# Block 1's back projection as seven half-size products, weight sums made in block 0's heads, and gamma and beta applied in the first state-space tiles

## The reference, cut to what matters

```python
def reference(x, ...):                    # x is 1 x 512 x 2048, fp32
    x = first_block(x, ...)
    return second_block(x, ...)

def first_block(x, w_in, ..., w_out, ln_g, ln_b):
    ...                                    # attention (8 heads), short convolution, pooling
    y = einsum('bse,ed->bsd', y, w_out)    # back projection, 512 x 2048 times 2048 x 2048
    return layer_norm(ALPHA * x + y, ln_g, ln_b)

def second_block(x, w_in, w_out, ..., ln_g, ln_b):
    ...                                    # sparse attention (8 heads), state-space mixer (4 groups)
    sub = einsum('bse,ed->bsd', mixed, w_out)
    return layer_norm(ALPHA_2 * h + sub, ln_g, ln_b)
```

## Time and profile before

| | us |
|---|---|
| median of 3 runs (1691.88 to 1692.17) | 1692.14 |
| the profiled execution's own time | 1692.62 |
| its span, first to last instruction | 1690.9 |
| PE busy in the span | 1677.5 (99%) |
| DVE, ACT, POOL busy | 914.2, 665.4, 716.4 |
| PE's granted clock, mean over the span | 0.998 |

### The profile page before, as it was taken

One profiled execution on the slowest core, in us unless ns is written; L12 is line 12 of the kernel. 1 busy time (PEld: TensorE's weight loads), 2 busy tenths in 40 slices (PEclk: granted clock), 3 DMA queues, 4 the chain that ended last, 5 costly groups with the idle time before them and its releaser, 6 DMA issues.

```text
span 1690.9 us, 21775 instructions
## 1 busy us (share of the span) xinstructions
PE 1677.5 (99%) x7902; PEld 1376.8 (81%) x7902; DVE 914.2 (54%) x1373; ACT 665.4 (39%) x917; POOL 716.4 (42%) x304
## 2 busy tenths in 40 slices
PE   9999999999999999999999999999999999999997
PEld 6888888888888888888888888887668888888886
DVE  6323312332455654988642754748789745556326
ACT  6434434443222225446642333424453545462220
POOL 4433343433444443446554434334235333326551
PEclk9999999999999999999999999999999999999999
DMA  6333233332577844765554342433123222217422
GB/s 238 114 93 92 89 93 94 93 94 82 202 289 292 296 150 139 244 229 185 172 172 156 92 134 87 137 105 119 61 77 100 75 87 75 87 50 275 135 89 100
DMA packets 67360, 232.31 MB, mean 137 GB/s; under 512 B 7336, under 2 KB 7592, under 8 KB 66000
## 3 DMA queue, kind: packets, MB, share of 16 engines
q1 hardware_dynamic: 59184, 206.33, 37.5%
q10 hardware_dynamic: 8096, 24.88, 4.1%
HBM read 205.93 MB, written 25.25 MB: 137 GB/s over the span
## 4 chain that ended last, share of the span: by engine, by line
PE 99%; DVE 1%; DMA 0%; issue 0%; SPq 0%; ACT 0%; DVEq 0%; ACTq 0%
PE bank L575 96%; PE bank L579 2%; DVE feats L1568 0%; DMA feats<-in_x_t 0%; DVE bank L1948 0%; DVE stats L1906 0%; DVE planes_lo L1579 0%; DVE planes_lo L1955 0%; ACT planes_hi L1105 0%; SPq L399 0%; SPq L401 0%; DVE mv L1935 0%; DVE rstd L1924 0%; DVEq L1933 0%; DVEq L1945 0%
## 5 line engine op out<-in xcount | busy, mean ns | idle before, releaser
L525 POOL TENSOR_TENSOR w_lo<-raw,w_hi 128x1024 fp32r<-128x1024 f32 x280 | 693.0, 2480 | 934.8 <-ACT w_hi L1060 934.8
L575 PE MATMUL bank<-planes_hi,w_hi 128*128 128x512 f32 (+1 forms) x1776 | 694.7, 391 | 1.1 <-ACT planes_hi L1105 0.7
L575 PE MATMUL bank<-planes_hi,w_lo 128*128 128x512 f32 (+1 forms) x1776 | 685.3, 386 | 0.0
L575 PE MATMUL bank<-planes_lo,w_hi 128*128 128x512 f32 (+1 forms) x1776 | 684.7, 386 | 0.1
L1060 ACT ACTIVATE w_hi<-raw 128x1024 fp32r<-128x1024 f32 x302 | 320.5, 1061 | 866.4 <-PE bank L575 813.0
L575 PEld LDWEIGHTS bank<-planes_hi,w_hi 128*128 128x128 f32 x1776 | 333.7, 188 | 84.2 <-issue 17.2
L575 PEld LDWEIGHTS bank<-planes_hi,w_lo 128*128 128x128 f32 x1776 | 333.6, 188 | 67.9
L575 PEld LDWEIGHTS bank<-planes_lo,w_hi 128*128 128x128 f32 x1776 | 333.9, 188 | 66.9 <-DVE planes_lo L1579 1.3
L575 PE MATMUL bank<-w_hi,planes_hi 128*128 128x512 f32 x368 | 143.7, 390 | 0.0
L575 PE MATMUL bank<-w_hi,planes_lo 128*128 128x512 f32 x368 | 143.3, 389 | 0.0
L575 PE MATMUL bank<-w_lo,planes_hi 128*128 128x512 f32 x368 | 143.2, 389 | 0.0
(11 more groups left out here) (336 smaller groups left out, 1630.1 us busy)
## 6 DMA issues: line engine op xcount, KB each, us to landing
raw<-in_stream SPq DMA_DIRECT2D x273, 512.0 KB, 3.6
raw<-sums_dram SPq DMA_DIRECT2D x32, 512.0 KB, 4.0
bias<-in_stream SPq DMA_DIRECT2D x10, 512.0 KB, 4.9
probs<-in_stream SPq DMA_DIRECT2D x10, 512.0 KB, 6.9
sums_dram<-bias SPq DMA_DIRECT2D x10, 512.0 KB, 5.2
sums_dram<-probs SPq DMA_DIRECT2D x10, 512.0 KB, 6.7
h_rows<-feats ACTq DMA_DIRECT2D x4, 1024.0 KB, 7.1
feats<-in_x_t SPq DMA_DIRECT2D x7, 512.0 KB, 8.9
```

The costliest lines, as they stand in the source:

```text
L525: nc.gpsimd.tensor_sub(w_lo[:, s, :], raw[:, s, :], w_hi[:, s, :].bitcast(fp32)).then_inc(lo_ready, count)
L575: return nc.tensor.matmul(o, a, b, start=start, stop=stop, skip_group_check=onto)
```

## The change

Block 1's back projection becomes seven half-size products too (`project_sevens2`): the halves A11, S3, S2, S4, S1, A22, A12 (`HALVES2`, each for two column pairs), 4 units each, 12 matmuls per unit, 56 units in all. The last half (units 52 to 55) is done row block by row block. The low parts of eight units (`SPLIT2`) are DVE's, those of the other 48 POOL's; `late_hi`, `late_lo`, `round_end` and `end_low_parts` go. `head_turn(15)` follows unit 3 and `head_pv(15)` unit 7 (before: units 1 and 3 of 24 matmuls).

The sums of block 1's planes that the scheme needs are made on DVE: S3's during head 9 (one TENSOR_TENSOR of 2048 elements), S2's, S4's and S1's in the back projection (`sum_planes2`), rounded by ACT (`cut_sum2`) and made low by DVE (`low_sum2`). DVE reads the banks half by half (`read_second`: two operations 128 x 512 per half, four for S1, and BN_STATS for the column blocks that are then whole), adds the parts common to two rows (`fold`) and runs `norm_rows` of row blocks 0 and 1 before it reads half 12.

The four sums of quarters of block 1's back weights are made in block 0's heads: 16 rounds (`sum_round`), two per head, each of four 256 KB loads, four TENSOR_TENSOR 128 x 512 on DVE and four 256 KB stores, all DMAs on SP's queue, to a new DRAM tensor. SP's load of the second pair of block 0's own sums (`load_pair(1)`) waits for the last stores.

Gamma and beta of block 0's norm are applied in the first state-space iteration: ACT loads halves of both (`load_affine`), DVE multiplies and adds eight times 128 x 1024 (`make_resid`) after `conv_tile(1)` and again after `conv_tile(3)`, and ACT stores the finished rows after tile 5 (`store_resid`), no longer right after the norm. ACT waits at tile 2 for the first half. What reads the space next (the rotation indices' DMA on ACT, `conv_tile(6)` on DVE) waits for those stores.

At block 1's back projection the stores of row blocks 0 and 1 are SP's, those of 2 and 3 ACT's.

```diff
-T_END = T_BACK2 + 16
+T_END = T_BACK2 + 28
...
+HALVES2 = [(of, pair) for of in ["A11", "S3", "S2", "S4", "S1", "A22", "A12"] for pair in range(2)]
+SET2_OF = [0, 1, 2, 3, 0, 1, 0, 1, 2, 3, 0, 1, 2, 3]
+STREAMED2 = {"A11": 0, "A12": 16, "S4": 24}
+SPLIT2 = [19, 23, 27, 29, 31, 35, 39, 43]
...
+            def store_round(unit, k, t):
+                sp.wait_ge(second_made, t + 1)
+                for i, of in enumerate(("S2", "S1", "A22", "S3")):
+                    sp.dma_start(sums2_dram[at(MADE_UNITS[of] + unit), :, S * k:S * k + S].rearrange("u p n -> p (u n)"),
+                                 wide[:, S * i:S * i + S]).then_inc(second_stored, 16)
...
+                if t == 1:
+                    sp.wait_ge(second_stored, 64 * 2 * UK)
...
-            low_parts(m0 + 1, ROUNDS - 1)
-            end_low_parts()
+            low_parts(m0 + 1, T_BACK2 // 2)
+            for n in range(UNITS):
+                tile = T_BACK2 + n // 2
+                if n not in SPLIT2:
+                    low_part(tile // 2, 2 * (tile % 2) + n % 2, 2 if n + 1 in SPLIT2 else 1)
...
+            def project_sevens2(after_unit):
+                for h, (of, pair) in enumerate(HALVES2):
+                    if h == 1:
+                        pe.wait_ge(feat_done, 31)
+                    if h == 3:
+                        pe.wait_ge(feat_done, 32)
+                    if h >= 4:
+                        before = max(g for g in range(h) if SET2_OF[g] == SET2_OF[h])
...
+                    for u in range(4):
+                        n = 4 * h + u
+                        wait_unit2(n)
+                        if of in ("S2", "S4", "S1"):
+                            part = [c for c in CUT2 if c[:2] == of and int(c[3]) < 2 * u + 2][-1]
+                            pe.wait_ge(sums_ready, len(CUT) + CUT2.index(part) + 1)
+                        elif of != "S3":
+                            pe.wait_ge(planes_ready, 48 + 2 * u + 2 if of == "A11" else 64)
+                        for i in range(2):
+                            last = unit_products2(h, n, i)
+                        last.then_inc(unit_used, 1)
+                        if n in after_unit:
+                            after_unit[n]()
...
-            project_back(1, T_BACK2, {1: lambda: head_turn(a), 3: lambda: head_pv(a, 1, B[0])}, {})
+            project_sevens2({3: lambda: head_turn(a), 7: lambda: head_pv(a, 1, B[0])})
...
+            def load_affine(half):
+                for i in range(2):
+                    act.dma_start(wide[:, HALF * i:HALF * i + HALF], ln1[i:i + 1, HALF * half:HALF * half + HALF].to_broadcast([P, HALF]))\
+                        .then_inc(ln1_loaded, 16)
...
+            def store_resid():
+                act.wait_ge(resid_made, 2)
+                for r in range(QB):
+                    act.dma_start(h_rows[P * r:P * r + P, :], row(r)).then_inc(rows_stored, 16)
...
+                    cut_second(EARLY[1], 8)
+                    head_exps(a)
+                    round_range(4, 7)
+                    round_probs(a)
                     act.wait_ge(rows_stored, STORED[0])
-                    load_resid(rows_in, 0)
-                    load_resid(rows_in, 1)
-
-                if blk:
-                    for db in range(4):
-                        cols = slice(S * db, S * db + S)
-                        act.dma_start(gamma1[db][:, :], ln1[0:1, cols].to_broadcast([P, S])).then_inc(ln1_loaded[db], 16)
-                        act.dma_start(beta1[db][:, :], ln1[1:2, cols].to_broadcast([P, S])).then_inc(ln1_loaded[db], 16)
+                    for i in range(2):
+                        act.dma_start(probs[:, 2 * i:2 * i + 2, :], col_blocks(2 + i, 0)).then_inc(resid_loaded[1], 16)
+                    round_back(7)
+                    act.wait_ge(feat_done, 31)
+                    cut_second(8, 12)
+                    round_back(8)
+                    cut_second(12, 15)
+                    round_range(9, 12)
+                    act.wait_ge(feat_done, 32)
+                    cut_second(15, KT)
                     act.dma_start(gamma, ln2[0:1, :].to_broadcast([P, D])).then_inc(ln_loaded, 16)
                     act.dma_start(beta, ln2[1:2, :].to_broadcast([P, D])).then_inc(ln_loaded, 16)
-                for db in range(4 if blk else 0):
-                    if db in (1, 2):
-                        act.wait_ge(rows_taken, 4 * db)
-                        load_resid(rows_in, db + 1)
-                    if db == 3:
-                        round_end()
...
+                    for i in range(2):
+                        act.dma_start(feats[:, 4 * (2 + i) + 1:4 * (2 + i) + 4:2, :], col_blocks(2 + i, 1)).then_inc(resid_loaded[1], 16)
+                    round_range(32, 52)
...
-                    for r in range(QB):
-                        store_z(r)
+                    act.wait_ge(unit_used, 2 * T_MISC)
+                    load_affine(0)
...
+                    root(0)
+                    round_back(52)
+                    root(1)
+                    round_range(53, 56)
+                    root(2)
+                    root(3)
+                    store_rows(2)
+                    store_rows(3)
...
+                    if it == 0 and k == SECOND_HALF_AT:
+                        act.wait_ge(resid_made, 1)
+                        load_affine(1)
+                    if it == 0 and k == 5:
+                        store_resid()
...
+            def sum_round(t):
+                dve.wait_ge(second_loaded, 64 * (t + 1))
+                b11, b12, b21, b22 = (wide[:, S * i:S * i + S] for i in range(4))
+                step(V.tensor_sub(b22, b22, b12))
+                step(V.tensor_sub(b12, b12, b11))
+                step(V.tensor_add(b11, b11, b22))
+                signal(V.tensor_sub(b21, b21, b11), second_made, t + 1)
...
                 head_softmax(a)
+                sum_round(2 * h - 2)
                 head_scale(a)
                 low_probs(a)
                 low_qk(h)
+                sum_round(2 * h - 1)
                 head_finish(a, a, a + 1, T_HEAD1 + 4 * a + 4)
...
+                    cut_second(8, 15)
+                    second_done(0)
+                    dve.wait_ge(resid_loaded[1], 64)
+                    read_second(0)
+                    head_finish(a, HEADS - 1, 32, T_HEAD2 - SK + 2 * HEADS, B[0])
+                    second_done(1)
+                    read_second(1)
+                    cut_second(15, KT)
+                    sum_planes2("S2 0:4")
+                    sum_planes2("S2 4:8")
+                    low_sum2("S2 0:4")
+                    low_sum2("S2 4:8")
+                    sum_planes2("S4")
+                    sum_planes2("S1")
+                    second_done(2)
+                    read_second(2)
+                    second_done(3)
+                    split_second(19)
+                    read_second(3)
+                    low_sum2("S4 0:4")
+                    low_sum2("S4 4:8")
+                    second_done(4)
+                    split_second(23)
+                    read_second(4)
+                    second_done(5)
+                    split_second(27)
+                    read_second(5)
+                    low_sum2("S1 0:4")
+                    low_sum2("S1 4:8")
+                    split_second(29)
+                    dve.wait_ge(resid_loaded[0], 64)
+                    fold(0)
+                    split_second(31)
+                    fold(1)
+                    dve.wait_ge(resid_loaded[1], 96)
+                    for h in range(6, 12):
+                        second_done(h)
+                        if h > 6 and 4 * h + 7 in SPLIT2:
+                            split_second(4 * h + 7)
+                        read_second(h)
+                    known2(0)
+                    known2(1)
                     dve.wait_ge(ln_loaded, 32)
-                    for r in range(QB):
-                        row_done(r)
-                        norm_rows(r)
+                    norm_rows(0)
+                    norm_rows(1)
+                    second_done(12)
+                    read_second(12)
+                    dve.wait_ge(rows_summed, 2)
+                    read_second(13, [0], 14)
+                    known2(2)
+                    norm_rows(2)
+                    second_done(13)
+                    read_second(13, [1], 15)
+                    known2(3)
+                    norm_rows(3)
             back_and_norm(0, T_BACK1)
...
+            def make_resid(half):
+                dve.wait_ge(ln1_loaded, 32 * (half + 1))
+                dve.wait_ge(rows_turned, 4 * QB)
+                for r in range(QB):
+                    part = half_row(r, half)
+                    step(V.tensor_mul(part, part, wide[:, 0:HALF]))
+                    ins = V.tensor_add(part, part, wide[:, HALF:D])
+                    if r < QB - 1:
+                        step(ins)
+                    else:
+                        signal(ins, resid_made, half + 1)
```

(85 more changed lines are left out.)

279 lines of the change are left out of this document (145 added, 134 removed).

## The result

The changed kernel takes 1696.12 us (median of 11 runs, 1695.36 to 1696.78) against 1692.17 us of the kernel before (11 runs, 1691.85 to 1693.39): ratio 1.0022, 95% interval 1.0013 to 1.0031. The forecast was 1697.

What follows compares the result with a forecast made beforehand. The prediction took PE to bound the kernel, with DVE's queue setting the end after the change. From 1692.62 us, +3.7 for the end and +1.0 for the state-space stage gave 1697.3, as run median 1697; range 1684 to 1703.

Steps and rivals of the forecast that it cites:

- The products: Block 1's back projection: 672 matmuls instead of 768, 96 fewer at 0.227 us each, -21.8 us on the path.
- The turns: DVE's two-SBUF-input operations and scalings exclude POOL's subtractions; cycles of 2.8, 3.35 or 4.4 us against PE's 2.72.
- head_turn(15): Turning of head 15: DVE's four scalings each wait for a POOL subtraction, so PE starts 4.8 us late.
- Unit 12: Back projection: plane cuts 8 to 14 take turns with POOL and ACT rounds unit 12 late, PE waits 5.0 us.
- Units 13 to 18: Back projection: DVE's two low sums of 1024 and two sums of 2048 take turns with POOL, +4.9 us.
- Units 54, 55: End of back projection: norms of row blocks 0 and 1 take turns with POOL's units 52 to 55, +0.5 and +2.0.
- The end: Behind the last matmul: DVE's remaining reads and norms end 16.2 us behind PE, balance +3.7 us.
- State-space stage: Gamma and beta applied there: the tile of 922.41 must wait for four 1 MB stores, 0 to +2, taken as +1.0 us.
- Heads: Weight sums in block 0's heads fit DVE's idle time: 0, bounds 0 and +2 us.
- A: Rival: the turns do not bite and PE stays fed, 1673.4 us; chance 0.13.
- B: Rival: the turns bite in part, the scalings or norms of rows 0 and 1 pass, 1684 to 1692 us; chance 0.20.
- C: Rival, the clock: PE pauses twice for 5 us and the granted clock leaves 1.00 before the end; chance 0.12.

Runs made afterwards that it cites:

- first experiment: The changed kernel with DVE's seven low cuts of planes 8 to 14 reading their first operand from an idle PSUM bank: 1691.13 us.
- fourth experiment: The changed kernel without the norm of row blocks 0 and 1, four operations of 8 columns left to signal: 1687.80 us.
- third experiment: The changed kernel with the low parts of units 5 and 6 made by DVE behind head 15's scalings instead of by POOL: 1692.43 us.

## Why the prediction was right, point by point

- **The products**: -21.8 us. From the first matmul of the back projection to the last it was 177.4 us before (1502.53 to 1679.96); after it is 173.5 (1502.13 to 1675.67), and without the 17.9 us of losses below 155.6: -21.8. Right. The losses are measured by how much further apart than 2.72 us two units start, so a restart and slow matmuls count in them.
- **The turns**: in the kernel before, of the four scalings of rows 6 only the first begins inside POOL's operation, and it takes 2.31 us; the three behind it take 0.29 each. The parts 0.55 and 2.15 us of the cycles are estimates: the operation alone (0.69 and 2.29) less the 0.14 by which 1.09 lies under 1.23. In after, POOL's three subtractions from 1529.51 on took 2.66, 2.85 and 2.84 us and the plane cuts beside them 2.79, 2.78 and 2.77 (2.8 laid out), the two low sums of 1024 from 1547.26 took 3.33 each (3.35), and the two sums of 2048 behind them 4.37 and 4.34 (4.4). What I took as free of POOL was so: BN_STATS of 128 x 512 took 0.69 us at 826.51 in the kernel before, inside a POOL subtraction (825.07 to 827.91), as did the operation on a bank ahead of it (825.78); two reductions of 128 x 256 and 128 x 384 took 0.42 and 0.55 inside another (106.96 to 109.37), as on average.
- **head_turn(15), +4.8:** PE's waits there are 1.6 and 1.9 us, and the half clock behind them costs about 1.5 us (7 matmuls 0.43 instead of 0.23 us apart): 5.4 with the restarts. The scalings and POOL excluded each other as said: 2.42, 2.20 and 2.25 us, each ending 0.15 to 0.28 us behind one of POOL's three subtractions, where in the kernel before such scalings take 0.35, 0.42 and 0.49 on average. I had all of it as waiting; nearly a third is clock.
- **Unit 12, +5.0:** measured 3.0. POOL's unit 12 was done 1.6 us earlier than laid out, and PE came 0.4 us later to it. Of this 1.1 us are the two DMA issues of gamma and beta: I had charged them with 1.94 us by the last two issues of ACT's timeline of before (1.10 in rows 9, and 0.84), and they took 0.35 and 0.45. The first experiment shows the cause of the wait.
- **Units 13 to 18, +4.9:** measured 0.5, 0.6, 0.6, 1.7, 1.6 and 0.6 us: 5.7. The turns of a sum of 2048 hit units 16 and 17, not 15 and 16.
- **Units 19 to 51, 0 to +2:** measured 0.4 and 0.3 us at units 29 and 31, and some 0.1s: 1.2.
- **Units 54, 55, +2.5:** waits of 0.4 and 1.6, with restarts 2.7.
- **Sum of PE's losses:** 17.9 us measured, 17.2 predicted. The errors inside it (-2.0 at unit 12; +0.6, +0.8, +1.2 and +0.2 elsewhere) nearly cancelled, and that is luck: the sum was better than its terms.
- **The end, +3.7:** The norm of row block 1 ended at 1673.8 (1673.6 laid out) and DVE at 1691.6 (1691.4), 16 us behind PE; +3.9. The fourth experiment shows that eight norm operations of row blocks 0 and 1 stood in it.
- **State-space stage, +1.0:** wrong, it cost 0: the last store had landed by 925.3, at the early end of my 925 to 931, and PE had until 933. That made the forecast 1 us too high.
- **Heads, 0:** right. In the head of rows 15 the idle time before the next bank fell from 17.57 to 12.29 and from 7.44 to 2.16 us, so the second round has little to spare:

```profile
325.49 0.29 DVE L1728 COPY probsT<-bank 128x128 f32<-128x128 f32 x1 [12.29 <-PE bank L616]
...
332.74 2.77 DVE L1683 TENSOR_TENSOR wide<-wide 128x512 f32<-128x512 f32 x1
...
338.39 0.69 DVE L1711 TENSOR_TENSOR feats<-bank,gate 128x512 f32 x1 [2.16 <-PE bank L612]
```

- **Rivals.** A and B did not come; C (a half clock behind PE's pauses) came in part, 3 us at half clock where I had said a chance of 0.12, and so did the sign that I had named as speaking against the forecast, a granted clock that leaves 1.00 before the end. By the timelines its price of 1.5 us did not reach the end, for PE waited 2.8 us before unit 12 behind it; no run takes the half clock alone away, so what C adds to the time is not shown. The kernel before had the half clock only behind its last matmul (0.50 from 1685 on the earlier trace rows). In after it came behind one of the two pauses: behind the one from 1513 to 1518 the clock was 0.50, behind the 2.8 us before unit 12 it stayed 1.00. Length alone does not separate the cases here (see the last section).

## What to carry to other kernels

When fewer matmuls make the units shorter, work out for each unit what the feeding engines need, and count VectorE's operations with two SBUF inputs, and its scalings, and GpSimd's operations as one queue (beside GpSimd the plane cuts took 2.14 us on average instead of 0.72, a scaling 2.2 to 2.4 instead of 0.35 to 0.49): here it was full for a time although the page has the engines busy 63% and 45% (and a wait for the other engine counts as busy in that: a scaling of 0.35 us stands there with 2.42). Where they meet at a moment when a unit is due, move one of them so that GpSimd has a lead, or let VectorE do GpSimd's part, which takes it half the time (1.23 against 2.40 us); the same work in another order, with other units on VectorE, was worth 12 us. And follow the last engine, not the busiest: VectorE ended 8 us behind the last matmul before and 16 after, and that gave back over a third of what the shorter product took off.

## What the runs showed that was not expected

- An operation of 8 columns waits as long for GpSimd as one of 1024 (2.3 us in the fourth experiment, where two such took 0.49 together with GpSimd idle; one of 1024 took 3.3 instead of 1.28).
- How long PE pauses does not alone tell whether the half clock follows. It followed 3.5 us in two parts (after), 4.2 us before unit 12 (third experiment) and 2.1 us before unit 12 (fourth; the rows below, columns as in the table by stretch of after), but not 2.8 us before unit 12 (after). It lasted 3 to 6 us and cost 0.2 us per matmul.

```profile
1543.00:1546.00 3.00, 1.29 (x6) 0.75 (x4) 2.97 (x2) 2.91 (x4) 2.60 (x1) 1.00 1.01 423
...
1548.00:1549.00 1.00, 1.00 (x4) 0.81 (x3) 1.00 (x1) 0.97 (x2) 1.00 (x1) 0.50 0.87 348
```
